# Seven half-size gate products in place of eight in three feed-forward layers of an fp32 decoder kernel

## The reference, cut to what matters

```python
def conv_ffn(h, w_up, w_gate, conv_w, conv_b, w_down):
    u = h @ w_up
    g = h @ w_gate
    g = lax.conv_general_dilated(g, conv_w[:, None, :].astype(g.dtype), window_strides=(1,),
                                 padding=[(CONV_WIDTH - 1, 0)],
                                 ...
    return (jax.nn.silu(g) * u) @ w_down
```

## Time and profile before

| | us |
|---|---|
| median of 3 runs | 2367.95 |
| lowest, highest | 2367.5, 2369.76 |
| span of the profiled execution | 2366.1 |

### The profile page before, as it was taken

The page is one execution under the profiler, slowest core; times in us unless marked ns, Lnnn a source line. Parts: engine busy times, 40 slices in busy tenths (PEclk is TensorE's granted clock), DMA queues, the critical chain, the costliest instruction groups (busy, mean ns, idle before and its releaser), DMA issues.

```text
span 2366.1 us, 38617 instructions
## 1 busy us (share of the span) xinstructions
PE 2351.2 (99%) x15330; PEld 2066.3 (87%) x15330; DVE 1093.8 (46%) x1680; ACT 852.4 (36%) x1319; POOL 909.6 (38%) x379
## 2 busy tenths in 40 slices
PE   9999999999999999999999999999999999999999
PEld 8898999999999999989988888867667888888887
DVE  5876353573443524555734535353463337422222
ACT  4335343332222324544322224454464333322222
POOL 2221223354444442223444444432224554444443
PEclk9999999999999999999999999999999999999999
DMA  5211222232222332112222323322213333232232
GB/s 193 72 64 37 78 77 81 80 99 97 89 89 89 98 103 64 46 46 72 90 98 89 98 90 106 109 65 67 85 54 98 107 115 108 91 101 94 96 98 89
DMA packets 60535, 208.13 MB, mean 88 GB/s; under 512 B 6762, under 2 KB 9428, under 8 KB 60420
## 3 DMA queue, kind: packets, MB, share of 16 engines
q1 hardware_dynamic: 56624, 202.01, 26.6%
q10 hardware_dynamic: 3796, 4.45, 0.6%
HBM read 204.24 MB, written 2.12 MB: 87 GB/s over the span
## 4 chain that ended last, share of the span: by engine, by line
issue 60%; POOL 24%; PE 15%; POOLq 1%; DVE 0%; DVEq 0%
POOL wl L2654 24%; PE ps L407 14%; PE ps L342 1%; POOLq L2653 0%; POOLq L2658 0%; POOLq L2654 0%; PE ps L503 0%; DVE X L478 0%; POOL Yf L2657 0%; POOL eps L2647 0%; DVEq L478 0%; POOLq L2883 0%
## 5 line engine op out<-in xcount | busy, mean ns | idle before, releaser
L2654 POOL TENSOR_TENSOR wl<-raw,wh 128x1024 fp32r<-128x1024 f32 x372 | 908.8, 2446 | 1440.0 <-ACT wh L445 1439.3
L445 ACT ACTIVATE wh<-raw 128x1024 fp32r<-128x1024 f32 x376 | 395.2, 1054 | 744.4 <-PE ps L407 507.3
L407 PE MATMUL ps<-Hh,wh 128*128 128x264 f32 (+2 forms) x1736 | 480.6, 325 | 1.9 <-DVE arena L2595 1.9
L407 PE MATMUL ps<-Hh,wl 128*128 128x264 f32 (+2 forms) x1736 | 480.6, 325 | 0.0
L407 PE MATMUL ps<-Hl,wh 128*128 128x264 f32 (+2 forms) x1736 | 480.6, 325 | 0.0
L407 PEld LDWEIGHTS ps<-Hh,wh 128*128 128x128 f32 x1736 | 291.7, 188 | 30.6 <-issue 2.3
L407 PEld LDWEIGHTS ps<-Hh,wl 128*128 128x128 f32 x1736 | 291.1, 188 | 28.1
L407 PEld LDWEIGHTS ps<-Hl,wh 128*128 128x128 f32 x1736 | 291.0, 188 | 27.2
L360 PE MATMUL ps<-Hh,wh 128*128 128x264 f32 (+1 forms) x1056 | 276.7, 326 | 1.6 <-DVE Yl L950 0.7
L360 PE MATMUL ps<-Hh,wl 128*128 128x264 f32 (+1 forms) x1056 | 255.4, 306 | 0.0
L360 PE MATMUL ps<-Hl,wh 128*128 128x264 f32 (+1 forms) x1056 | 255.4, 306 | 0.0
(11 more groups left out here) (263 smaller groups left out, 2831.7 us busy)
## 6 DMA issues: line engine op xcount, KB each, us to landing
raw<-in_w_all SPq DMA_DIRECT2D x376, 512.0 KB, 3.5
X<-in_xT SPq DMA_DIRECT2D x4, 528.0 KB, 8.9
arena<-scratch ACTq DMA_DIRECT2D x2, 1024.0 KB
arena<-in_extra ACTq DMA_DIRECT2D x2, 528.0 KB
out<-X SPq DMA_DIRECT2D x1, 1024.0 KB, 4.3
out<-X SPq DMA_DIRECT2D x4, 256.0 KB, 2.0
arena<-in_extra ACTq DMA_DIRECT2D x2, 264.0 KB
cst<-in_consts SPq DMA_DIRECT2D x1, 448.0 KB, 11.5
```

Source lines behind the costliest of these rows:

```text
L407: mm = pe.matmul(ps[:, 2 * j + h + bank, 0:c1 - c0], w[:, j, k, :], moving(x, blk, c0, c1), start=(at == 0 and part == 0), stop=(at == len ...
L445: act.activation(wh[:, j], raw[:, j], ACT.Copy).then_inc(hi_split, 1)
L2654: pool.tensor_tensor(wl[:, j], raw[:, j], wh[:, j].bitcast(F32), ALU.subtract).then_inc(split_ready[j], 1)
```

## The change

Trips 2 to 9 (counting from 0; `FOLDED`) of each layer are folded. The gates of a trip are a 2 x 2 matrix of weight quarters (4 blocks of input by one block of output) times a 2 x 2 matrix of x quarters (4 blocks by one half of the tokens). In place of eight quarter products it makes seven, in Winograd's form: four have sums of weight quarters, four sums of x quarters. The x sums and their parts are made once in a layer: ScalarE scales and copies x in the norm (`gained_x`), VectorE adds (`summed_x`) and makes the low parts (`summed_x_lo`). The weight sums are made in each folded trip by VectorE (`sum_forms`). Partial products are combined through PSUM accumulation, three copies by ScalarE and additions by VectorE.

The down units of two trips' outputs are spread over the folded trips: four down groups of four blocks a trip, between the gate forms and the up halves. The order of the 15 forms of 512 elements each is `FORMS`. Their high and low parts go through a ring of ten slots: ScalarE makes a form's high part once the form ten places earlier is done, and GpSimd makes all low parts. The folded trips are written out, not looped. Trips 0, 1 and 10 stay as before but share the code with the new work, and the last six blocks of down follow trip 10 as before.

```diff
-CHUNKS = [(0, 8), (8, 8), (16, 6)]
+TRIPS = FB // 2
+FOLDED = range(2, 10)
+FORMS = ("P1", "P5", "P2", "P6", "P3", "d0", "P7", "d1", "u0a", "u0b", "P4", "d2", "u1a", "u1b", "d3")
+SUMS = ("P5", "P6", "P3", "P7")
+NF = len(FORMS)
+RING = 10
+FOLD_UNITS = 6 * len(FOLDED)
...
-        for c, (_, n) in enumerate(CHUNKS):
-            add(f"ffn{l}_up{c}", 4, n // 2)
-            add(f"ffn{l}_down{c}", 4, 2)
+        add(f"ffn{l}_up0", 4, 2)
+        add(f"ffn{l}_up2", 4)
...
+                if folding is not None:
+                    gained_x(act, folding, b)
...
+        def gained_x(act, l, b):
+            d, (T, _), off = ffn_views(l), FFN_T[l], FFN_OFF[l]
+            W = T // 2
+            for h, dst in enumerate((d["xs"][0], d["b12"]) if b < 4 else (d["xs"][3], d["xs"][2])):
+                x = X[:, b, off + h * W:off + h * W + W]
+                ins = act.activation(dst[:, b % 4], x, ACT.Copy, scale=param(FFN_GAIN[l], b))
+            sig["x_gained"].by(ins)
+        def summed_x_hi(act, l):
+            d = ffn_views(l)
+            for q in range(4):
+                sig["x_summed"].take(act, "act")
+                n_hi.by(act.activation(d["xh"][q], d["xs"][q], ACT.Copy))
+        def summed_x(v, l):
+            d = ffn_views(l)
+            n1, n2, t3, t4 = d["xs"]
+            sig["x_gained"].take(v, "dve", 4)
+            sig["x_summed"].by(v.tensor_tensor(n1, n1, d["b12"], ALU.subtract))
+            sig["x_summed"].last(v)
+            sig["x_gained"].take(v, "dve", 4)
+            sig["x_summed"].by(v.scalar_tensor_tensor(out=n2, in0=n1, scalar=-1.0, in1=t3, op0=ALU.mult,
+                                                      op1=ALU.subtract))
+            sig["x_summed"].last(v)
+            sig["x_summed"].by(v.tensor_tensor(t3, t3, d["b12"], ALU.subtract))
+            sig["x_summed"].by(v.scalar_tensor_tensor(out=t4, in0=n2, scalar=-1.0, in1=t4, op0=ALU.mult,
+                                                      op1=ALU.subtract))
+            sig["x_summed"].last(v)
+        def summed_x_lo(v, l, q):
+            d = ffn_views(l)
+            n_hi.take(v, "dve")
+            h_ready.by(v.tensor_tensor(d["xl"][q], d["xs"][q], d["xh"][q].bitcast(F32), ALU.subtract))
+        def plain_act(act, l, t):
+            T, TU = FFN_T[l]
+            d = ffn_views(l)
+            st, i = (PLAN[f"ffn{l}_up0"], t) if t < 2 else (PLAN[f"ffn{l}_up2"], 0)
+            if t == 1:
+                summed_x_hi(act, l)
+                fold_hi(act, l, d, 0), fold_hi(act, l, d, 1)
+                for b in range(2):
+                    act.wait_ge(unit_done[d["js"][b]], unit(st, b, i)[1])
+                    fold_hi(act, l, d, 2 + 2 * b), fold_hi(act, l, d, 3 + 2 * b)
+            else:
+                split_after(act, st, range(2), i)
+            for mm in range(2):
+                plain_silu(act, l, d, mm, st, i)
+            for mm in range(2):
+                j, k = unit(st, 2 + mm, i)
+                if t == 1:
+                    act.wait_ge(unit_done[j], k)
+                    fold_hi(act, l, d, 6 + 2 * mm), fold_hi(act, l, d, 7 + 2 * mm)
+                if t != 1 or mm == 0:
+                    act.wait_ge(acc_free[j], k)
+                    product_hi(act, l, d, 2 * t + mm)
+                if t != 1:
+                    split_hi(act, j, (k + 1) * 16)
...
+        def plain_dve(v, l, t):
+            T, TU = FFN_T[l]
+            d = ffn_views(l)
+            rs = rs_view(T)
+            st, i = (PLAN[f"ffn{l}_up0"], t) if t < 2 else (PLAN[f"ffn{l}_up2"], 0)
+            if t == 1:
+                summed_x_lo(v, l, 0)
+                summed_x_lo(v, l, 1)
+                sum_forms(v, l, d, 0)
+            for mm in range(2):
+                j, k = unit(st, mm, i)
+                v.wait_ge(unit_done[j], k)
+                g = d["gs"][:, mm, 2:] if l < 2 else d["c1"][:, mm]
+                v.tensor_tensor(cols(g, T), acc(j, T), cols(rs, T), ALU.mult).then_inc(acc_free[j], 1)
+                if l < 2:
+                    v.wait_ge(acc_free[j], k)
+                    gate_conv(v, l, d, 2 * t + mm)
+            if t == 1:
+                summed_x_lo(v, l, 2)
+                summed_x_lo(v, l, 3)
+            for mm in range(2):
+                gate_scaled(v, l, d, mm)
+                dve.last(v)
+                j, k = unit(st, 2 + mm, i)
+                v.wait_ge(unit_done[j], k)
+                v.tensor_tensor(cols(d["c1"][:, mm], TU), acc(j, TU), cols(d["sg"][:, mm], TU), ALU.mult)\
+                 .then_inc(acc_free[j], 1)
+            for mm in range(2):
+                j, k = unit(st, 2 + mm, i)
+                v.wait_ge(acc_free[j], k)
+                product_lo(v, l, d, 2 * t + mm)
+            y_ready.last(v)
+        def sum_forms(v, l, d, r):
+            G = len(FOLDED) * l + r
+            for q in ("g0", "g1"):
+                v.wait_ge(fold_landed[q], 16 * (G + 1))
+            if r:
+                lows_made(v, l, r - 1, "P7")
+            a11, a12, a21, a22 = (d["pair"][:, q] for q in range(4))
+            s3, s1, s2, s4 = (d["ws"][:, q] for q in range(4))
+            sig["w_summed"].by(v.tensor_tensor(s1, a21, a22, ALU.add))
+            sig["w_summed"].by(v.tensor_tensor(s3, a11, a21, ALU.add))
+            v.wait_ge(sig["w_summed"].sem, 4 * G + 1)
+            sig["w_summed"].by(v.tensor_tensor(s2, a11, s1, ALU.add))
+            sig["w_summed"].last(v)
+            sig["w_summed"].by(v.tensor_tensor(s4, a12, s2, ALU.add))
+            sig["w_summed"].last(v)
+        def fold_hi(act, l, d, f):
+            r, name = f // NF, FORMS[f % NF]
+            G = len(FOLDED) * l + r
+            if f >= RING:
+                forms_done(act, l, f - RING)
...
+            sig["form_hi"].by(act.activation(d["slots"][f % RING][0], d["from"][name], ACT.Copy))
+        def fold_pool(pool, l):
+            d = ffn_views(l)
+            for r in range(len(FOLDED)):
+                for i, name in enumerate(FORMS):
+                    f = NF * r + i
+                    pool.wait_ge(sig["form_hi"].sem, l * NF * len(FOLDED) + f + 1)
+                    hi, lo = d["slots"][f % RING]
+                    sig["form_lo"].by(pool.tensor_tensor(lo, d["from"][name], hi.bitcast(F32), ALU.subtract))
...
+                sp.dma_start(raw[:, j].rearrange("p k c -> p (k c)"), w_all[at]).then_inc(fold_landed[q], 16)
+            for r in range(len(FOLDED)):
+                at = u + 6 * r
+                def plain_split(b):
+                    sp.wait_ge(split_ready[js[b]], unit(st, b, 1)[1])
+                if r:
+                    sp.wait_ge(sig["w_summed"].sem, 4 * (len(FOLDED) * l + r))
+                    lows_made(sp, l, r - 1, "P4")
+                else:
+                    plain_split(0)
+                into("g0", js[0], at)
+                if r == 0:
+                    plain_split(1)
+                into("g1", js[1], at + 1)
+                if r:
+                    lows_made(sp, l, r - 1, "u1b")
+                    into("u", js[3], at + 2)
+                    lows_made(sp, l, r - 1, "d3")
+                    into("d", js[2], at + 3)
+                else:
+                    plain_split(2)
+                    into("d", js[2], at + 3)
+                    plain_split(3)
+                    into("u", js[3], at + 2)
+                lows_made(sp, l, r, "d1")
+                into("d", js[2], at + 4)
+                lows_made(sp, l, r, "u0b")
+                into("u", js[3], at + 5)
...
+        def fold_act(act, l):
+            d, (T, TU) = ffn_views(l), FFN_T[l]
+            W = T // 2
+            for r, t in enumerate(FOLDED):
+                G = len(FOLDED) * l + r
+                for i, name in enumerate(FORMS):
+                    if name in ("P1", "P6"):
+                        forms_done(act, l, NF * r + i)
+                        act.wait_ge(sig["end_free" if name == "P1" else "mid_free"].sem, G)
+                        sig["trunk_copied"].by(act.activation(d["s1" if name == "P1" else "s2"],
+                                                              ps[:, d["trunk"][r % 2], 0:W], ACT.Copy))
+                    if r == 0 and name == "P1":
+                        j, k = unit(PLAN[f"ffn{l}_up0"], 3, 1)
+                        act.wait_ge(acc_free[j], k)
+                        product_hi(act, l, d, 3)
+                    if name == "P5":
+                        forms_done(act, l, NF * r + i)
+                        act.wait_ge(sig["corner_done"].sem, G)
+                        sig["mid_copied"].by(act.activation(d["s5"], ps[:, d["mid"], 0:W], ACT.Copy))
+                    f = NF * r + i + RING
+                    if f < NF * len(FOLDED):
+                        fold_hi(act, l, d, f)
+                    elif i >= 8 and i % 2 == 0:
+                        forms_done(act, l, NF * r + i)
+                        j, n = unit(PLAN[f"ffn{l}_up2"], (i - 8) // 2)
+                        split_hi(act, j, n * 16)
```

(80 more changed lines are left out.)

386 lines of the change are left out of this document (274 added, 112 removed).

## The result

The changed kernel takes **2371.49 us** (median of 20 runs, 2369.75 to 2373.37); the kernel before, in the same sessions, 2368.72 (20 runs). The ratio is 1.0013, 95% interval 1.0007 to 1.0019: slower by about 3 us, within the 0.2% called no change. The forecast was 2375, range 2350 to 2390. The profiled span grew by 4.7 us, from 2366.1 to 2370.8.

What follows compares the result with a forecast made beforehand. TensorE was taken to bound the kernel. The span of 2366.1 us less 29.4 gain, plus 33.0 loss at the folded trips' starts and 3.6 clock, gave 2373.3; with 1.85 from span to median, 2375, range 2350 to 2390.

Steps and rivals of the forecast that it cites:

- Gain: Folded trips: one gate product in eight removed; 11.5 us each in layers 0 and 1, 6.4 in layer 2; 29.4 altogether.
- Rival D: Forms on TensorE: single-bank products of 264 columns go slower than 0.120 us; 20 us more, 2395; chance 0.07.
- The alternation of VectorE and GpSimd: Folded trips' start: SBUF instructions of the two engines wait each other out; layer 0 lengthened by +4.3, +4 and +4.4 us.
- VectorE's queue: Layer 0, norm to product of trip 1's first up unit: 33.1 us without lock, just fitting P6's start.
- The lateness of P6: First folded trip, layer 0: P6 starts at 519.9, 12.6 us late, behind VectorE's product and ScalarE's copy of P1.
- The clock behind P6: Layers 0 and 1: TensorE's clock may fall after standing 8.3 us before P6; 1.8 us a layer, 3.6 altogether.
- u0a's wait: First folded trip, layer 0: u0a waits 1.8 us for d0's residual, after the late second u load and P6's copy.
- Layer 2: Folded trips' start in layer 2: no convolution, queue 10 us shorter, so a loss of only 2.8 us.
- Hidden elsewhere: Norm's scaled copies on ScalarE, end of the last folded trip and removed chunk ends: cost 0.
- A: Folded trips' starts: the lock bites seldom; loss 4 to 14 us, no clock loss, median 2343 to 2353; chance 0.14.
- B: Starts cost half to four fifths of the forecast, clock stays; loss 21 to 30 us, 2360 to 2368; chance 0.22.
- C: Steady folded trips: d0's residual comes late for u0a; 0.5 us in each of 24 trips adds 12, 2387; chance 0.17.

Runs made afterwards that it cites:

- the run with short low parts: Changed kernel with GpSimd's low-part instructions cut to an eighth where folded trips start, most low parts left out, measurement only: 2342.00 us, 0.9893 of the kernel before.
- the filled run: Changed kernel plus 36 spare TensorE products before P6 in the first folded trip of layers 0 and 1: 2370.62 us, 1.0011 of the kernel before.
- the run with the short P7: Changed kernel with P7 making only 3 of its 12 products in every folded trip: 2359.80 us, 0.9969 of the kernel before.
- the other moves: Changed kernel with all x-sum work before the norm's wait, ScalarE's copies ahead of high parts, next gate loads ahead of second u load: 2341.68 us, ratio 0.9889.
- the copies first: Changed kernel with ScalarE's copies of P1 and P5 ahead of rounding trip 1's first product: 2372.61 us, 1.0019 of the kernel before.
- both copies freed: Changed kernel with all x-sum work before the norm's wait, P1 and P5 copies first, u1a's high part behind P6's copy: 2351.85 us, ratio 0.9932.
- x in the norm: Changed kernel with the x sums, their high parts and low parts all made before the wait for the norm's factors: 2353.52 us, ratio 0.9939.

## Why the prediction was right

The number is 3.5 us from the median and the case is the one called likeliest: the gain is whole in the steady trips and goes where they start. It landed in the lower part of that case's range (2368 to 2382), so that "slower", given 0.48, did not come out clear of 0.2%. That it came so near is in part luck, as the errors below have both signs. Step by step:

- **Gain, 29.4 forecast, 28.0 measured.** Layer 0: 11.5 and 11.8. The steady trip was forecast at 33.12 and takes 33.44, but before had the same excess (2304 products in 279.3 us are 0.1212 each, since down units take 5.85 to 5.87 us where 48 x 0.120 is 5.76), so it cancels. Layer 1: 11.5 and 10.2, as its down and up forms take 2.72 to 2.79 us, where half of a down unit took 2.72. Layer 2: 6.4 and 6.0; a form takes 1.41 to 1.44 us, so that 0.120 was right for 256 columns and 0.113 wrong. The semaphore waits of 15 forms, bounded by 6 us and taken as 0, are at most the 1.4 that is missing. Rival D falls.
- **The alternation of VectorE and GpSimd: right, in mechanism and in size.** Forecast for layer 0 (the lengthening of VectorE's instructions, in us): x sums +4.3, low product and x parts +4, the rest +4.4. Measured against the free durations: +4.3, +5.0 and +4.3. The first evacuation was forecast at 481.4 and started at 481.15. That the Trainium skill's lock (SBUF — State Buffer, Who interferes with whom) weighs on this change is what the run with short low parts shows: 29.5 us, with the loads that come earlier by it.
- **VectorE's queue: mis-sized.** 33.1 us without lock; 514.92 - 471.8 less 13.6 are 29.5. I took gaps of 0.15 us between VectorE's instructions from rows 7, and they are 0.03 to 0.05: evacuations and convolutions of a trip take 5.65 us and not 6.6. The same three instructions of the convolution, each waiting for the one before, are 0.14 to 0.17 us apart in the kernel before, which has them in a loop, and 0.04 in the changed one, which has them written out. That the loop does it was not tested. With the shorter queue the product was done 2.5 us before its forecast, and P6 started at 516.96, not 519.9.
- **The lateness of P6.** It came 9.7 us late (forecast 12.6). The text named 2.2 before trip 1 and 8.3 before P6, which make 10.5; for the other 2.1 its working gives no place (nor does 12.9 with a wait of 1.8 make the 15.1 at u0a). Measured: 2.0, 1.7 of slow clock in trip 1, and 5.9; in layer 1, 2.2 and 6.8. The fall of the clock behind trip 1's stand was not in the forecast at all.
- **The clock behind P6: right.** 1.8 us a layer forecast, 1.8 and 1.7 measured in P6 and P3. My reason for not taking the full 2.9, that the second u load takes part of it, is what the filled run shows for part of the saving; another is that the clock was back at 2.4 GHz within P3.
- **u0a's wait: right**, 1.8 forecast, 1.7 and 1.8 measured, with the releaser and the cause (the second u load, the copy behind it) as forecast.
- **Layer 2: mis-sized.** 2.8 us forecast, 5.1 measured. Trip 1's 2.3 was right (2.2) and P6 did not wait; but P7 stood 2.5 us for the copy of P6 behind that second u load, where I had 0.4. In layers 0 and 1 TensorE's own lateness hid this load; in layer 2 there was no such cover.
- **Hidden elsewhere: right.** Trip 1's stand in layer 0 begins 0.2 us from where trip 1 started before (480.05 and 479.82); the 16 copies in the norm cost nothing.
- **Rivals.** A, the lock bites seldom, gave 2343 to 2353: that is the time of the run in which GpSimd is out of the way (2342), so its price was right, its condition false. B fell, though narrowly in the cost: the starts took 31.4 of 36.6 forecast, six sevenths, where B ended at 30; but the clock did not stay, as B had it. C did not happen, but the run with the short P7 confirms its place and how near it was: room of about half a microsecond or less, where I had 1.0 and 0.7.

The errors partly cancelled: gain 1.4 too high, loss 5.2 too high, and 1.2 more by chance of the clock. The +7.2 of span in the forecast (2373.3 - 2366.1) became +4.7.

## What to carry to other kernels

A removed product is worth its pace only where the engines that feed it have room, so work out the first trip of a new regime by itself: here three first trips gave back all that 24 trips gained, and moving four VectorE instructions a layer ahead of a wait where the engine stood idle anyway turned the ratio from 1.0013 into 0.9958, and the other moves into 0.9889. Each move uncovered the next wait in line (copy, u load, weight sums), so a chain is to be followed until the first trip is as long as a steady one, and a single move that gains nothing (the copies first) is no proof that it was not needed (the wait of 0.8 us before P6 went only with it). Where VectorE and GpSimd both work from SBUF, place VectorE's long instructions where GpSimd is idle: two of the four sums took 3.33 and 3.44 us beside it, and 1.26 ahead of it.

## What the hardware showed

- GpSimd's form of 512 elements takes 1.08 us at least, 1.30 in the middle for forms out of `raw`, and 1.45 in the mean beside a busy VectorE (forecast 1.2); its unit of 1024 elements 2.34 at least. Halving the size about halves the time, but a unit of 128 elements still took 0.46 to 1.02, where an eighth of 2.34 is 0.29.
- The clock of the changed kernel fell behind a stand of TensorE of 2.1 us (trip 1 of layer 0; this and the next from the start of one product to the start of the next) and not behind longer ones (2.3 in layer 1, 2.5 in layer 2). Before P4 with both copies freed, stands of 2.4, 3.0 and 2.8 us left it at 2.4 GHz too, while those of 3.0 and 3.2 before P7, with x in the norm, did not. The same wait, ahead of the first feed-forward unit of one merge stage, 2.3 us long in both kernels, left the clock alone before and cost 1.2 us after:

```profile
1790.00:1795.00 5.00, 3.10 (x14) 1.00 0.57 170
```

```profile
1797.00:1801.00 4.00, 4.00 (x12) 0.57 0.47 154
```

The first is the kernel before, the second the changed one. The clock fell at that place in three of the eight experiments too and not in the others, and behind trip 1's stand of layer 2 in one. What decides it stays open.
